# Per-sample gates of a conditioned decoder layer: broadcast 512-column products replaced by 17-column products, split in three bf16 pieces, transposed and spread by a 0/1 matmul

## The reference, cut to what matters

```python
mod = jax.nn.silu(c) @ w_ada + b_ada                # (b, 6D), b = 1 prompt or 16 samples a core
sh1, sc1, g1, sh2, sc2, g2 = jnp.split(mod[:, None, :], N_MOD, axis=-1)
h = rms_norm(x) * (1 + sc1) + sh1
proj = h @ w_in                                     # then HGRN2 heads and a short convolution
...
mix = jnp.concatenate([o_rec, o_conv], axis=-1) @ w_out
x = x + g1 * mix
h2 = rms_norm(x) * (1 + sc2) + sh2
x = x + g2 * (jnp.square(jax.nn.relu(h2 @ w_up)) @ w_down)
```

## Time and profile before

| | |
|---|---|
| median of three runs | 885.97 us (863.92 to 1020.68) |
| the profiled execution | 868.4 us, its slowest core's span 866.8 us |
| spans of the other seven cores | 859.8 to 861.6 us |
| PE busy | 816.7 us, 94% of the span |
| DVE, ACT, POOL busy | 454.0, 369.8, 173.1 us |
| granted TensorE clock of the eight cores | 0.986 to 0.994 |
| DMA | 106.69 MB, mean 123 GB/s |

### The profile page before, as it was taken

One profiled execution on the slowest core, in us unless ns is written; L12 is line 12 of the kernel. 1 busy time (PEld: TensorE's weight loads), 2 busy tenths in 40 slices (PEclk: granted clock), 3 DMA queues, 4 the chain that ended last, 5 costly groups with the idle time before them and its releaser, 6 DMA issues.

```text
span 866.8 us, 16618 instructions; the slowest of 8 cores (859.8 to 866.8 us)
## 1 busy us (share of the span) xinstructions
PE 816.7 (94%) x5954; PEld 519.4 (60%) x6005; DVE 454.0 (52%) x876; ACT 369.8 (43%) x803; POOL 173.1 (20%) x231
## 2 busy tenths in 40 slices
PE   1579999999899999999999999999999999999996
PEld 1448876577676868656545654565456545644864
DVE  2366996386677876953015562456245624532422
ACT  3267953464566778447404331333133313310412
POOL 3110143252314331510013011101210111111002
PEclk9979999999899999999999999999999999999999
DMA  8999926988893339599995231213121122102001
GB/s 159 194 195 191 197 75 103 204 207 176 184 225 111 134 126 162 137 195 184 194 210 193 87 98 71 99 50 98 73 98 50 50 88 83 37 14 97 26 1 49
DMA packets 27341, 106.69 MB, mean 123 GB/s; under 512 B 3414, under 2 KB 4438, under 8 KB 22268
## 3 DMA queue, kind: packets, MB, share of 16 engines
q0 software_dynamic: 6624, 44.14, 30.6%
q1 hardware_dynamic: 18908, 55.46, 19.1%
q10 hardware_dynamic: 1728, 6.03, 2.2%
HBM read 123.93 MB, written 22.68 MB: 169 GB/s over the span
## 4 chain that ended last, share of the span: by engine, by line
PE 85%; DMA 6%; DVE 3%; issue 2%; ACT 1%; POOL 1%; another core or an unknown queue 0%; ACTq 0%; DVEq 0%; POOLq 0%
PE B L510 83%; DMA adaf<-w_ada 5%; PE B L521 2%; DMA St<-srec 1%; ACT W L537 1%; DVE W L548 1%; DVE Sd L544 0%; DVE W L554 0%; POOL mix L544 0%; DVE Ts L544 0%; DVE W L544 0%; DVE hT L550 0%; DVE sg L554 0%; DVE sm L544 0%; DVE mix L544 0%
## 5 line engine op out<-in xcount | busy, mean ns | idle before, releaser
L510 PE MATMUL B<-h2T,wup 128*128 128x384 bf16 (+1 forms) x1536 | 240.2, 317 | 0.0
L510 PE MATMUL B<-wdn,uT 128*128 128x512 bf16 (+1 forms) x1095 | 234.7, 373 | 1.3
L510 PE MATMUL B<-hT,win 128*128 128x256 bf16 (+1 forms) x1728 | 198.3, 272 | 6.4 <-DMA win<-w_in 5.0
L510 PEld LDWEIGHTS B<-h2T,wup 128*128 128x128 bf16 x1536 | 149.5, 98 | 83.8
L537 ACT ACTIVATE W<-B 128x384 f32<-128x384 f32 (+2 forms) x209 | 103.7, 497 | 207.6 <-PE B L510 186.2
L510 PEld LDWEIGHTS B<-wdn,uT 128*128 128x128 bf16 x1120 | 109.2, 98 | 122.6
L510 PEld LDWEIGHTS B<-hT,win 128*128 128x128 bf16 x1728 | 161.0, 100 | 29.1 <-issue 6.6
L544 POOL TENSOR_TENSOR xr<-xr,W 128x512 f32<-128x512 f32 x63 | 83.4, 1328 | 296.7 <-DVE W L544 262.4
L544 DVE TENSOR_TENSOR W<-B,Gp 128x512 f32<-128x512 f32 (+1 forms) x65 | 44.2, 681 | 159.8 <-PE B L510 159.6
L544 DVE TENSOR_TENSOR uT<-W,B 128x384 bf16<-128x384 f32 (+1 forms) x160 | 83.7, 525 | 77.9 <-ACT W L537 71.7
L537 ACT ACTIVATE W<-xr 128x1024 bf16<-128x1024 f32 (+2 forms) x19 | 18.4, 967 | 144.6 <-POOL xr L544 139.9
(11 more groups left out here) (156 smaller groups left out, 653.8 us busy)
## 6 DMA issues: line engine op xcount, KB each, us to landing
x<-xr SPq DMA_DIRECT2D x17, 512.0 KB, 11.4
xn<-x SPq DMA_DIRECT2D x17, 512.0 KB, 4.3
xr<-x SPq DMA_DIRECT2D x17, 512.0 KB, 3.5
ada<-w_ada POOLq DMA_DIRECT2D x8, 1024.0 KB, 15.5
xr<-xp SPq DMA_DIRECT2D x16, 512.0 KB, 8.2
wup<-w_up POOLq DMA_DIRECT2D x8, 1024.0 KB, 14.6
wdn<-w_down POOLq DMA_DIRECT2D x8, 1024.0 KB, 39.4
yp<-xr SPq DMA_DIRECT2D x15, 512.0 KB, 2.6
```

The costliest lines, as they stand in the source:

```text
L510: ins = e.matmul(o_, lhsT=l_, rhs=r_, start=st, stop=sp_, skip_group_check=True)
```

## The change

All gates are made in one way. For each half of 512 channels `gate_rows` multiplies with the weight block as the weights and the 17 columns of `scT` moving (4 times 8 matmuls of 17 columns), which gives the gate with channels on partitions. DVE adds the bias there (`gT`, 128 by 68), rounds to bf16, subtracts, and does so again: three bf16 pieces (`gpc`), whose sum is the fp32 number. Four transposes bring them to 51 rows (3 pieces of 17) of 512 channels, ACT copies them to SBUF (`grow`) and SP writes them to DRAM. `select` is then one matmul of 512 columns over 51 partitions whose weights are 0 and 1: it adds the three pieces of the wanted row and puts it on the wanted partitions. For the samples, and for g2, the 51 rows are first read back from DRAM into a buffer of the `xr` ring (`fetch_rows`), and the weights are spread by DVE (`spread`). The bias rows, POOL's eight copies and the loads of the spread gates are gone.

```diff
-    def gate_half(bi, g, half, gt, gt_n):
+    def gate_rows(bi, g, half, dst, dst_n):
         t, n = ada_slot[bi]
         bank, bn = DR.take()
-        mm([(bank[0:17, :], scT[:, k, :], t[:, k, :], k == 0, k == 7) for k in range(8)], [n, "scT"], [bn])
...
+        for cj in range(4):
+            mm([(bank[:, cj * 17:cj * 17 + 17], t[:, k, cj * 128:(cj + 1) * 128], scT[:, k, :], k == 0, k == 7) for k in range(8)],
+               [n, "scT"], [bn])
+        j0 = (16 if g == 0 else 40) + 4 * half
+        g3 = gT[:].rearrange("p (a b) -> p a b", b=17)
+        tt("dve", g3, bank[:, 0:68].rearrange("p (a b) -> p a b", b=17), badaT[:, j0:j0 + 4].unsqueeze(2).to_broadcast([128, 4, 17]),
+           ALU.add, [bn, "vecT"], ["gT"])
+        for i in range(3):
+            pc = gpc[:].rearrange("p (a c) -> p a c", c=51)[:, :, 17 * i:17 * i + 17]
+            copy("dve", pc, g3, ["gT"], ["gpc#%d" % i])
+            if i < 2:
+                tt("dve", g3, g3, pc, ALU.subtract, ["gT", "gpc#%d" % i], ["gT"])
+        bank, bn = DR.take()
+        Mb = bank[:, :].bitcast(BF16)
+        tr([(Mb[0:51, cj * 128:(cj + 1) * 128], gpc[:, cj * 51:(cj + 1) * 51], ident) for cj in range(4)], ["gpc", "cB"], [bn])
+        copy("act", dst, Mb[0:51, 0:512], [bn], [dst_n])
+        dma("sp", rows_d[g][:, half * 512:(half + 1) * 512], dst, [dst_n], ["rows%d_%d" % (g, half)], 51 * 1024)
+
+    def fetch_rows(g, buf):
...
+        dma("sp", v, rows_d[g], ["rows%d_0" % g, "rows%d_1" % g], [xn], 51 * 2048)
...
+    def select(row, row_n, half, banks, sel=None):
+        G, gn = (Gs, "Gs") if sel else (Gp, "Gp")
+        bank, bn = banks.take()
+        lhs, ln_ = sel if sel else (selb[0:51, 0:1].to_broadcast([51, 128]), "selb")
+        mm([(bank[:, :], lhs, row, True, True)], [ln_, row_n], [bn])
+        copy("act", G[:, half * 512:(half + 1) * 512], bank[:, :], [bn], ["%s#%d" % (gn, half)])
...
-    gates_wide(False)
+    for half in range(2):
+        gate_rows(4 + half, 0, half, grow[0:51, :], "grow")
+        select(grow[0:51, :], "grow", half, DR)
...
-    gates_wide(True)
+    rw = fetch_rows(0, xrR.take())
+    sel = spread(WT.take())
+    for half in range(2):
+        select(rw[0][:, half * 512:(half + 1) * 512], rw[1], half, DR, sel)
...
             if n_ == 3 and step == "G":
-                gates(1)
+                for half in range(2):
+                    gate_rows(10 + half, 1, half, grow1[0:51, half * 512:(half + 1) * 512], "grow1#%d" % half)
                 load_states()
...
-            load_gates(1, prompt=False)
+            sel = spread(WB.take())
+            for half in range(4):
+                select(rw[0][:, half % 2 * 512:(half % 2 + 1) * 512], rw[1], half % 2, GB, sel if half > 1 else None)
```

More of the change, by code:

```diff
@@ L495, in assemble @@
     x1_d = nc.dram_tensor("x1", [17, 128, 1024], F32, kind="Internal").ap()
-    gate_d = nc.dram_tensor("gates", [17, 2048], F32, kind="Internal").ap()
+    rows_d = nc.dram_tensor("rows", [2, 51, 1024], BF16, kind="Internal").ap()
     kv_d = nc.dram_tensor("kvs", [2, 128, 512], BF16, kind="Internal").ap()
@@ L650, in assemble @@
     ubR = Ring("ub", 2, [128, 2, 260])
-    bgr = one("bgr", [128, 512], BF16, offset=at["p"])
+    grow = one("grow", [128, 512], BF16, offset=at["p"])
     ucar = one("ucar", [128, 4, 32]); uco = one("uco", [128, 4, 32])
@@ L657, in assemble @@
     vecT = one("vecT", [128, 72]); scT = one("scT", [128, 8, 17], BF16)
+    gpc = one("gpc", [128, 204], BF16); gT = one("gT", [128, 68])
     at["p"] = max(at["p"], a0 + 7 * 8192)
@@ L711, in assemble @@
     vOR = Ring("vo", 1, [128, 512], BF16, offset=at["p"] + 3072)
+    grow1 = one("grow1", [128, 1024], BF16, offset=at["p"])
     mix_slot(2, at["p"])
@@ L820, in gates_wide @@
[L820 to L827, removed]
-        for half in range(2):
-            t, n = ada_slot[4 + half]
-            bank, bn = DR.take()
-            specs = []
-            for k in range(8):
-                lhs = ex[:, k, :] if sample else scT[:, k, 0:1].to_broadcast([128, 128])
-                specs.append((bank[:, :], lhs, t[:, k, :], k == 0, False))
-            specs.append((bank[:, :], selb[0:4, half:half + 1].to_broadcast([4, 128]), bgr[0:4, :], False, True))
-            mm(specs, [n, "scT", "selb", "bgr"] + ([exn] if sample else []), [bn])
-            copy("act", G[:, half * 512:(half + 1) * 512], bank[:, :], [bn], ["%s#%d" % (gn, half)])
@@ new lines, in spread @@
+    def spread(buf):
+        x, xn = buf
+        v = x[:].bitcast(BF16)[0:51, 0:128]
+        copy("dve", v.rearrange("p (s t) -> p s t", t=8), selb[0:51, 1:17].unsqueeze(2).to_broadcast([51, 16, 8]), ["selb"], [xn])
+        return v, xn
+    def select(row, row_n, half, banks, sel=None):
[4 more added lines that the diff above has]
+        copy("act", G[:, half * 512:(half + 1) * 512], bank[:, :], [bn], ["%s#%d" % (gn, half)])
@@ L1451, in assemble @@
             if step == "R" and n_ + 1 == len(tiles):
+                rw = fetch_rows(1, xrR.take())
                 got = [fetch2(blk) for blk in bgroups[1][:2]]
```

44 lines of the change are left out of this document (10 added, 34 removed).

## The result

The changed kernel takes 885.1 us (884.9 to 886.8), the kernel before 863.8 to 863.9 us beside it: a ratio of 1.023 (95% interval 1.020 to 1.027; the two times alone would give 1.025), 2.3% slower. Executions that were disturbed, as those of 885.97 and 1020.68 us of the kernel before, are left out of the comparisons. I had forecast 864 us, in a range of 856 to 882.

The account below looks back on a forecast made before the run. PE was taken as the bound, except DVE from 110 to 130 us. Terms +2.0 + 1.0 - 3.9 - 4.5 = -5.4, with +1.0 for the clock, gave -4.4 us from 868.4: 864.0 us, range 856 to 882.

Parts of the forecast that it names:

- Stores and the read-back: Prompt's second selection: wait for the first store, 0 to 3.2 us, taken as +1.0; no wait at the samples' selection.
- the rule on the outer dimension: Stores of 51 rows: 3 engines with 17 rows each; if it holds, the read-back rival gains.
- The slow rival: Samples' selection: two stores and read-back in turn make PE wait 11 to 19 us, 877 to 883 us; chance 0.2.
- The prompt's g1: 110 to 135 us, DVE the bound: +1.1 added work, +1.9 new wait, -1.0 DVE lead; +2.0, between -1.6 and +3.0.
- The saving of 2.66 us: Prompt's g1 products on PE: shorter by 2.66 us between recurrence steps that wait for DVE, counted as nothing.
- The new wait: Second transposes of the prompt's g1: PE waits 1.9 us for the third CAST on DVE.
- its +1.0 behind two new waits: Behind two new waits of 1 to 2 us: part of the lowered clock's cost, between 0 and 2.2, taken as +1.0.
- Samples and g2: Samples' g1 and g2, PE leading: 3.64 and 0.30 us less PE work, -3.9 us.
- the whole PE sum: All gates on PE: 12.2 us removed and 6.7 added, 5.5 us less if PE were the bound throughout.
- The weight loads: 17-column products: loads overlap at 25 ns per product; rival counting them in full, 9.1 us more, 873; chance 0.02.
- The states: Near 232 us: the samples' states load comes earlier, removing the wait and its lowered clock; -4.5 us, between 0 and -4.5.

Follow-up runs that it names:

- e2: The changed kernel with 52 rows instead of 51 in every copy, store and read-back, same order and single buffer: 873.1 us, ratio 1.012.
- e4: The changed kernel without the four DVE steps that make the second and third bf16 pieces of g1, otherwise same order: 883.5 us, ratio 1.024.
- e3: The changed kernel with 8 overwritten 512-column products ahead of each half's narrow ones for the prompt's g1: 884.0 us, ratio 1.025.
- e8: The prompt's g1 as in the kernel before, the samples' g1 (rows in SBUF) and g2 the new way, planned anew: 868.5 us, ratio 1.005.
- e9: The kernel before with only the samples' g1 made the new way, rows kept in SBUF, planned anew: 872.1 us, ratio 1.005.
- e11: The changed kernel with g1's rows in SBUF, two ACT neighbours exchanged and 8 overwritten wide products per half of the prompt's g1: 873.4 us, ratio 1.007.
- e5: The changed kernel with g1's rows kept in SBUF, without their two stores and read-back, otherwise same order: 874.2 us, ratio 1.012.
- e12: e5 with the next tile's norm steps moved behind the work at hand on ACT and DVE: 867.7 us, ratio 1.006.

## Why the prediction was wrong, point by point

**The step that failed: "Stores and the read-back".** I put +1.0 us, between 0 and 3.2, on ACT's second copy waiting for the first store. The place was right, down to the engine and the buffer; the size was 8.88 us and some 2.5 us of lowered clock behind it. My upper end took the slowest small store shown, 14.1 us for 128 KB, as a bound for 51 KB (the 1.8 us of 64 KB at my lower end are a load, `ucar<-sconvT`, not a store); the store took 18.4. (By its own terms the end would be 136.6 - 134.5 = 2.1 us, or 3.0 with ACT's copy; 3.2 does not come out of them.) Bytes were the wrong measure: 52 rows instead of 51 are more bytes, and land in time (e2). The number of packets that go one behind the other between larger ones of the weight loads decided, and the rule on the outer dimension (3 engines for 51) stood only beside a rival. That the two `ada` loads would be in flight just then I had read from the changed order, and charged 1 us for it.

**The slow rival** had the sign and, with 877 to 883 us, nearly the size, at a chance of 0.2. It had slow transfers among the `ada` loads right, but the wrong one: the read-back, which I gave 24.5 us, was not waited for; the first store was. That it comes near 885 is in part luck, since the waits for `mix` and `Sb` were in none of the cases.

**The prompt's g1, +2.0 (-1.6 to +3.0).** From transposes to transposes it is 59.7 against 56.0 us, +3.7 (3.0 to 4.7 over the cores), mostly over my upper end. The saving of 2.66 us did count as nothing, and the transposes and the selection that were added there did count, 0.75 us. The new wait was not the one I named: for the prompt's g1 the third CAST was not waited for in the changed kernel, and e4 shows that the split is not the cost there; it is waited for, 0.85 us instead of my 1.9, only where the clock stays up (e3). With less to do between the steps of the recurrence PE waited 0.97 and 1.31 us for it and was busy for 7.2 of 10 us, and the clock went down to the lower of its two levels (at 116.8 us, before the second of these waits), for which my sum had only a part of its +1.0 behind two new waits: 16 matmuls take 2.85 us that take 1.92 at full clock. The same core by stretch:

```profile
110.00:116.80 6.80, 5.52 (x89) 4.45 (x87) 6.80 (x13) 5.33 (x11) 2.29 (x3) 1.00 0.43 114
116.80:123.60 6.80, 5.29 (x59) 3.78 (x56) 6.80 (x19) 4.64 (x10) 4.76 (x9) 0.50 0.00 0
```

e8 leaves the wide products there and has none of this. The last link, that the missing work alone brings the clock down, is supported by e3 (the clock stays at 1.00 with wide work) and not shown further; e3 also shows that holding the clock up by such work does not save the time.

**Samples and g2, -3.9, and the whole PE sum, -5.5.** PE's own pace fell by 4.5 us, 1.0 less than the sum. The weight loads cost nothing: 32 products in 0.82 us (155.51 to 156.33 above, from start to start).

**The states, -4.5.** The wait is gone as I said. But it was not in the times that the changed kernel was compared with. The profile before was of its slowest core; the other seven cores of that same execution, at 860 to 862 us, wait 0 us for the states. The kernel's times in the comparison are 863.8 to 863.9, and my sum should have started there instead of at 868.4, and without this term: 863.9 + 2.0 + 1.0 - 3.9 + 1.0 = 864.0. The two mistakes cancel, so they are not why the forecast failed. Whether the slow cores of the kernel before on the chip of e9 to e11 waited for the states is not shown.

**Nothing was in the sum for the order's side effects**: the wait for `mix`, about 6 us with the clock behind it (7.5 to 1.0 in the table, e5 to e12), and the wait of 1.94 us for `Sb` at 201 us. I compared the two orders where the change was made, not at the next places where ACT and DVE stand behind a load.

## What to carry to other kernels

The store's latency under load went with how many of its packets queued one behind the other (17, or 4 by the rule), not with its bytes: so count a transfer's streams before its bytes, try an outer dimension with a larger divisor (one row more won 1.1% here), and give a buffer that is stored from a second copy if anything in order stands behind its reuse. Work that an engine does while it waits for another can be free: here 2.66 us less of it gained nothing, and the clock went down. Putting other work in its place did not bring the time back (e3, e11). With a planner that reorders everything, look for each in-order engine at what stands behind every load that comes late, and read a wait on the slowest core against the other cores before counting on its removal.

## What the runs showed of the hardware that was not expected

A CAST of 128x68 on DVE took 0.19 to 0.20 us alone and 1.29 us when it met an addition on POOL, on all eight cores of e8, near 143 us. First DVE, then POOL, core 5:

```profile
142.09 0.20 DVE L564 CAST gpc<-gT 128x68 bf16<-128x68 f32 x1
...
143.12 1.29 DVE L564 CAST gpc<-gT 128x68 bf16<-128x68 f32 x1
...
214.90 2.87 DVE L564 CAST gpc<-gT 128x68 bf16<-128x68 f32 x1
```

```profile
143.09 1.26 POOL L544 TENSOR_TENSOR xr<-xr,W 128x512 f32<-128x512 f32 x1 [1.97 <-DVE gT L544]
...
214.59 0.59 POOL L571 DMA_DIRECT2D St<-srec  x1 [4.43 <-PE B L510]
215.21 2.49 POOL L544 TENSOR_TENSOR xr<-xr,W 128x512 f32<-128x512 f32 x2
```

It ends when the addition ends. The one at 214.90 began while POOL was still issuing a load, and lasted over the two additions right behind it, with PE idle for 2.29 us until DVE came free; on five cores, where no addition followed that issue at once, the CAST ended with the issue, after 0.28 to 0.29 us. The Trainium skill, page "SBUF — State Buffer", section "SBUF: two separate sides", describes the port pair that VectorE, in some of its modes or with two inputs from SBUF, shares with GpSimd as an exclusive lock for the whole instruction. The ends of both rows agree; which mode the CAST ran in no run here shows. A step priced at 0.2 us can so cost fourteen times that, by what runs on another engine.
